# Work of VectorE moved within a layer: bonus factors, low halves, value LoRA shift, mod sums and the banks of the output projection

## The reference, cut to what matters

```python
for l in range(DEPTH):                                  # DEPTH = 2
    mod = (silu(c) @ w_mod[l] + b_mod[l])               # 6 vectors of 1024
    sh1, sc1, gt1, sh2, sc2, gt2 = split(mod, 6)
    h = rmsnorm(x, norm1_g[l]) * (1 + sc1) + sh1
    z = h @ w_cat                                       # layer 1 has 32 more columns: the value LoRA
    ya = rglru_branch(z[LX], z[LY], ...)                # A: conv, gated linear recurrence
    yb = diff_attention(z[Q], z[K], z[V], ...)          # B: rope, two softmax maps
    yc, v_first = rwkv7_mix(z[RW], ..., zvd=z[VD], ...) # C: below
    merged = (sigmoid(z[0:D]) * (ya @ w_merge_a[l]) + sigmoid(z[D:2*D]) * (yb @ w_merge_b[l])
              + sigmoid(z[2*D:3*D]) * (yc @ w_merge_c[l]))
    x = x + gt1 * (merged @ w_out[l])
    h2 = rmsnorm(x, norm2_g[l]) * (1 + sc2) + sh2
    u = causal_dwconv(h2 @ w_up, conv_w, conv_b)        # width 3, 6144 channels
    x = x + gt2 * ((gelu(u[gate]) * u[val]) @ w_down)
return rmsnorm(x, final_g)

# in rwkv7_mix, layer 1: the value's mix with that of layer 0
v = v + (v_first - v) * sigmoid(v0 + token_shift_mix(zvd, v_mu) @ v2)
out = wkv7_scan(r, decay, k, v, -kk, kk * a)            # the state
out = groupnorm(out) * lnx_g + lnx_b
bonus = sum(r * k * r_k, per head) * v
y = (out + bonus) * g
```

## Time and profile before

| | |
|---|---|
| time, median of 3 executions | 1196.32 us (1192.1 to 1197.6) |
| profiled execution: its own time | 1199.33 us |
| its span in the trace | 1197.5 us |
| TensorE busy | 1151.9 us (96%) |
| VectorE busy | 842.9 us (70%) |
| ScalarE busy | 567.7 us (47%) |
| GpSimd busy | 60.2 us (5%) |
| HBM read | 212.01 MB |
| mean granted TensorE clock | 0.978 |

### The profile page before, as it was taken

How to read it: one execution, slowest core, us unless ns; L and a number is a source line. 1 busy time by engine, 2 the same in 40 slices (tenths; PEclk the granted TensorE clock), 3 DMA queues, 4 the chain that set the end, 5 groups by cost and what they waited for, 6 DMA issues and landing times.

```text
span 1197.5 us, 24198 instructions
## 1 busy us (share of the span) xinstructions
PE 1151.9 (96%) x10160; PEld 1043.8 (87%) x10160; DVE 842.9 (70%) x1246; ACT 567.7 (47%) x867; POOL 60.2 (5%) x104
## 2 busy tenths in 40 slices
PE   6999999999999999999999899999999999999997
PEld 6889888888788999999988698778887889999996
DVE  5468988477475788885535679876765767888763
ACT  2236547622264666652331274575124556666532
POOL 0000010003000000001000000000030000000000
PEclk9799999999999999998999899999999999999999
DMA  9956454234135466667725435441521545445650
GB/s 378 297 204 217 176 177 189 94 142 143 72 141 212 156 242 218 227 226 278 281 85 186 173 142 189 156 183 72 199 86 71 189 190 184 175 178 187 225 184 36
DMA packets 40951, 214.34 MB, mean 179 GB/s; under 512 B 7680, under 2 KB 8064, under 8 KB 21536
## 3 DMA queue, kind: packets, MB, share of 16 engines
q1 hardware_dynamic: 29344, 171.13, 39.0%
q0 software_dynamic: 11520, 41.95, 10.0%
HBM read 212.01 MB, written 1.05 MB: 178 GB/s over the span
## 4 chain that ended last, share of the span: by engine, by line
PE 83%; DVE 11%; issue 3%; DMA 3%; ACT 1%; SPq 0%; DVEq 0%; ACTq 0%
PE ps L1587 13%; PE ps L1589 13%; PE ps L1588 13%; PE ps L1600 8%; PE ps L1762 6%; PE ps L1760 6%; PE ps L1766 6%; PE ps L1864 4%; DVE RLO L1091 2%; DMA mring<-wmod_dram 2%; PE ps L1558 2%; PE ps L1565 2%; DVE macc L987 2%; PE ps L1549 1%; PE ps L2040 1%
## 5 line engine op out<-in xcount | busy, mean ns | idle before, releaser
L845 ACT ACTIVATE WH<-ring 128x1024 fp32r<-128x1024 f32 x144 | 151.6, 1058 | 185.7 <-PE ps L1589 170.0
L1459 DVE TENSOR_TENSOR WLO<-ring,WH 128x1024 fp32r<-128x1024 f32 x144 | 175.1, 1223 | 91.2 <-ACT WH L845 91.2
L1587 PE MATMUL ps<-HH,WH 128*128 128x256 f32 x736 | 208.3, 283 | 0.0
L1588 PE MATMUL ps<-HL,WH 128*128 128x256 f32 x736 | 208.3, 283 | 0.0
L1589 PE MATMUL ps<-HH,WLO 128*128 128x256 f32 x736 | 208.3, 283 | 0.0
L1587 PEld LDWEIGHTS ps<-HH,WH 128*128 128x128 f32 x736 | 141.3, 192 | 0.0
L1588 PEld LDWEIGHTS ps<-HL,WH 128*128 128x128 f32 x736 | 141.3, 192 | 0.0
L1589 PEld LDWEIGHTS ps<-HH,WLO 128*128 128x128 f32 x736 | 141.3, 192 | 0.0
L1587 PE MATMUL ps<-GH,WH 128*128 128x256 f32 x384 | 110.6, 288 | 0.0
L1588 PE MATMUL ps<-GL,WH 128*128 128x256 f32 x384 | 109.4, 285 | 0.0
L1589 PE MATMUL ps<-GH,WLO 128*128 128x256 f32 x384 | 109.4, 285 | 0.0
(11 more groups left out here) (383 smaller groups left out, 2494.5 us busy)
## 6 DMA issues: line engine op xcount, KB each, us to landing
ring<-wmain_dram SPq DMA_DIRECT2D x150, 1024.0 KB, 4.8
mring<-wmod_dram POOLq DMA_DIRECT2D x80, 512.0 KB, 5.0
G<-wmod_dram SPq DMA_DIRECT2D x3, 1024.0 KB, 7.8
R<-wmod_dram SPq DMA_DIRECT2D x3, 1024.0 KB, 15.6
TK<-wmod_dram SPq DMA_DIRECT2D x2, 1024.0 KB, 20.7
X<-x_t_dram SPq DMA_DIRECT2D x1, 1024.0 KB, 9.8
SW<-small_dram SPq DMA_DIRECT2D x2, 512.0 KB, 12.6
y_dram<-H SPq DMA_DIRECT2D x4, 256.0 KB, 2.2
```

Source lines behind the costliest of these rows:

```text
L845: A(WH[:, n % 2, part], ring[:, b, part], ACT.Copy).then_inc(hi_ready, 1)
L1459: V.tensor_tensor(WLO[:, n % 2, part], ring[:, b, part], WH[:, n % 2, part].bitcast(F32), ALU.subtract).then_inc(lo_ready, 1)
L1587: MM(out, w_high[:, at], high, start=start, stop=False, skip_group_check=True)
L1588: MM(out, w_high[:, at], low, start=False, stop=False, skip_group_check=True)
```

## The change

- In the preamble VectorE takes block 15 itself (`DIRECT` loses it), reads sum 0 before block 14 instead of after 15, and reads sum 1 ahead of the sixth column of H instead of the fourth. The matmuls that nobody reads are five ahead of `mod_sum(0)` and five ahead of `mod_sum(1)` (they were 2, 2 and 3 in three places).
- The shift of the value LoRA in layer 1 moves ahead of the shift of V.
- The factors of the bonus and of the norm leave the attention part and come in the state chain, behind the chunk of step c = 0 and of step c = 1. The low halves of pairs 16 to 19 each move one rotation forward, the two mod blocks too, and two of them move behind the first four chunks.
- `FILL_READ` is 12.
- The output pairs take banks 0 to 3 in the order of their number.
- In the down stage of layer 0 the sums 5, 6 and 7 come behind other pairs (2, 4 and 9 instead of 0, 3 and 10), and one mod block moves.

```diff
+    if OU <= k < UP:
+        return [k - OU]
     return [g % 4]
...
-FILL_TURN, FILL_READ, FILL_CHAIN, FILL_OUT, FILL_NORM = 8, 8, 4, 6, 8
+FILL_TURN, FILL_READ, FILL_CHAIN, FILL_OUT, FILL_NORM = 8, 12, 4, 6, 8
...
-DIRECT = (3, 7, 11, 15)
+DIRECT = (3, 7, 11)
 UP_BLOCKS = [0] * 4 + [1, 0] * 10
-DN_BLOCKS = [[2, 2, 2, 2, 1, 1, 1, 1, 1, 1, 0, 0], [1, 1, 1, 1, 1, 1, 1, 1, 0, 0, 0, 0]]
-DN_SUMS = [{0: 5, 3: 6, 10: 7}, {8: 11}]
+DN_BLOCKS = [[2, 2, 2, 2, 2, 1, 1, 1, 1, 0, 0, 0], [1, 1, 1, 1, 1, 1, 1, 1, 0, 0, 0, 0]]
+DN_SUMS = [{2: 5, 4: 6, 9: 7}, {8: 11}]
...
             for n in range(FIRST):
+                if n == FIRST - 2:
+                    mod_vector(0)
                 if n not in DIRECT:
                     mod_block(n)
-            mod_vector(0)
...
-                    if (n, m) == (0, 4):
+                    if (n, m) == (0, 6):
                         mod_vector(1)
...
                 half_pairs_low(2, 4)
+                if l:
+                    dve.wait_ge(zv_up, 2)
+                    zv = RT[0:32, :]
+                    V.tensor_tensor(YB[0:32, 2, 1:S], zv[:, 0:S - 1], zv[:, 1:S], ALU.subtract).then_inc(step, tick(n_step))
+                    V.tensor_scalar(YB[0:32, 2, 0:1], zv[:, 0:1], -1.0, None, ALU.mult).then_inc(step, tick(n_step))
+                    after()
+                    V.scalar_tensor_tensor(YB[0:32, 2, :], YB[0:32, 2, :], PR[0:32, l, COL["vmu"]:COL["vmu"] + 1], zv,
+                                           ALU.mult, ALU.add).then_inc(zv_ready, 1)
...
                 mod_vector(6 * l + 2)
                 if l:
-                    dve.wait_ge(zv_up, 2)
-                    zv, zd = RT[0:32, :], Acol
-                    V.tensor_tensor(YB[0:32, 2, 1:S], zv[:, 0:S - 1], zv[:, 1:S], ALU.subtract).then_inc(step, tick(n_step))
-                    V.tensor_scalar(YB[0:32, 2, 0:1], zv[:, 0:1], -1.0, None, ALU.mult).then_inc(step, tick(n_step))
-                    after()
-                    V.scalar_tensor_tensor(YB[0:32, 2, :], YB[0:32, 2, :], PR[0:32, l, COL["vmu"]:COL["vmu"] + 1], zv,
-                                           ALU.mult, ALU.add).then_inc(zv_ready, 1)
...
-                    if b == 0:
-                        dve.wait_ge(lora_act, 10 * (l + 1))
-                        dve.wait_ge(bon_ready, 2 * (l + 1))
-                        for j in range(4):
-                            V.scalar_tensor_tensor(BON[:, j, :], BON[:, j, :], col(l, "lnb", j), GG[:, j, :], ALU.add, ALU.mult).then_inc(gg_ready, 1)
-                        dve.wait_ge(gg_ready, 8 * l + 4)
-                        for j in range(4):
-                            V.tensor_scalar(GG[:, j, :], GG[:, j, :], col(l, "lng", j), None, ALU.mult).then_inc(gg_ready, 1)
+                    if b < 2:
+                        half_pairs_low(16 + 2 * b, 18 + 2 * b)
                     if 0 < b < 3:
-                        half_pairs_low(14 + 2 * b, 16 + 2 * b)
-                    if b:
                         mod_beside(2)
...
                 dve_chunks(0, 4)
+                mod_beside(2)
                 read_scores(0)
...
                         dve_chunks(26 + c, 27 + c)
+                    if c == 0:
+                        dve.wait_ge(lora_act, 10 * (l + 1))
+                        dve.wait_ge(bon_ready, 2 * (l + 1))
+                        for j in range(4):
+                            V.scalar_tensor_tensor(BON[:, j, :], BON[:, j, :], col(l, "lnb", j), GG[:, j, :], ALU.add, ALU.mult).then_inc(gg_ready, 1)
+                    if c == 1:
+                        dve.wait_ge(gg_ready, 8 * l + 4)
+                        for j in range(4):
+                            V.tensor_scalar(GG[:, j, :], GG[:, j, :], col(l, "lng", j), None, ALU.mult).then_inc(gg_ready, 1)
...
-                    keep_clock(2, 5, X[:, 0, :])
+                    keep_clock(5, 5, X[:, 0, :])
                     mod_sum(0)
-                    keep_clock(2, 5, X[:, 0, :])
                     mod_direct(11)
-                    keep_clock(3, 5, X[:, 0, :])
-                    mod_direct(15)
+                    keep_clock(5, 5, X[:, 0, :])
                     mod_sum(1)
...
                     if a == 0:
-                        emptied(g, g % 4)
+                        emptied(g, j)
...
                         down(1, q)
+                        if 4 + q in DN_SUMS[l]:
+                            mod_sum(DN_SUMS[l][4 + q])
```

More of the change, by code:

```diff
@@ L359, in residual_ps @@
         def residual_ps(g, j, i):
-            return ps[:, 5, 0:S] if (j, i) == (3, 1) else ps[:, g % 4, i * S:(i + 1) * S]
+            return ps[:, 5, 0:S] if (j, i) == (3, 1) else ps[:, banks_of(g)[0], i * S:(i + 1) * S]
         def duo(b):
@@ L549, in squares @@
                         g = PAIRS * ((n - 1) // 2) + (OU if n % 2 else PAIRS - 4) + m // 2
-                        act.wait_ge(bank_free[g % 4], EMPTIED[g][g % 4] + 1)
+                        at = banks_of(g)[0]
+                        act.wait_ge(bank_free[at], EMPTIED[g][at] + 1)
                     A(H[:, m, :], X[:, m, :], ACT.Square).then_inc(x_sq, 1)
@@ L1448, in residual @@
                         V.scalar_tensor_tensor(X[:, m, :], residual_ps(g, j, i), scale[:, m:m + 1], X[:, m, :],
-                                               ALU.mult, ALU.add).then_inc((x_tile, bank_free[g % 4])[i], 1)
+                                               ALU.mult, ALU.add).then_inc((x_tile, bank_free[banks_of(g)[0]])[i], 1)
                 g0 = PAIRS * l + UP
```

## The result

| | before | changed |
|---|---|---|
| median | 1196.96 us (1192.1 to 1201.09, 4 executions) | 1216.41 us (1211.54 to 1218.47, 4 executions) |
| ratio | | 1.0158, 95% interval 1.0108 to 1.0209 |
| profiled execution, own time / span | 1199.33 / 1197.5 us | 1217.9 / 1216.1 us |
| mean granted TensorE clock | 0.978 | 0.962 |
| TensorE busy | 1151.9 us | 1169.6 us |

The forecast was 1183.3 us; the kernel became 19 us slower. Of the cases written down it is rival 4: the state chain dropped to the half clock, and stayed there nearly to its end. The rival had been given 0.05.

A forecast was written before the change was run, and what follows sets the result against it. TensorE was taken as the bound (83% of the chain of waits); gains and losses 4.5 + 7.0 - 7.0 + 0 + 0.3 + 8.2 = 13.0 us less, from a median of 1196.32 to 1183.3 us, range 1175 to 1192.

The forecast's parts named there:

- rival 4: State chain, once dropped, stays at 1.2 GHz until the norm; 20 us added to the forecast, 1203 us; chance 0.05.
- State chain: FILL_READ 12 makes TensorE wait 1.9 and 1.8 us for chunks' low halves: 3.5 us a layer, 7.0 us lost.
- rival 3: Each of the four new state chain waits drops the clock for about 6.7 us, half chain: 1190 us; chance 0.12.
- Value LoRA: Layer 1, shift moved ahead: TensorE's wait only changes its name, to the read of a sum; 0 us.
- Down stage: Layer 0, sums 6 and 7 behind other pairs: no late-block wait and less half clock; 8.2 us gained.
- Attention part: Both layers: TensorE's waits for low halves go, until VectorE is late next; 2.8 and 4.2, 7.0 us gained.
- together I put 3.2 us there in place of the 2.42: Attention part: VectorE's waits for DMA and ScalarE after the move, 3.2 us against 2.42 us before.
- Preamble: VectorE adds block 15, so the first product starts at 33.1 with the clock full; 4.5 us gained.
- rival 1: The preamble keeps the half clock, gaining 0.8 us at best there: 1187 us; chance 0.28.
- Banks: Output pairs: out(0) starts earlier, then VectorE is late for out(1); 0.3 us gained in layer 0, none in layer 1.
- The chain's small waits left the clock full: State chain: the argument written against rival 4, whose chance was 0.05.

The follow-up runs named there:

- after_early: The changed kernel, FILL_READ still 12, with the low halves of chunks 26 to 29 made one step of the chain earlier: 1183.60 us, ratio 0.9922.
- before_value: The kernel before with only the value LoRA's shift ahead of the V shift and the read of mod sum 8 right behind it: 1188.36 us, ratio 0.9956.
- before_bonus: The kernel before with only the eight bonus and norm factor instructions moved from the first rotation to the state chain: 1185.49 us, ratio 0.9954.
- before_banks: The kernel before with only the output pairs in banks 0 to 3 in order, and their readers: 1191.43 us, ratio 0.9978.
- before_read12: The kernel before with FILL_READ 12 instead of 8 alone: 1213.84 us, ratio 1.0156.
- before_attention: The kernel before with the whole attention edit: bonus instructions in the state chain, low halves of pairs 16 to 19 and mod blocks moved: 1190.35 us, ratio 0.9984.
- before_preamble: The kernel before with only the preamble's edit: 1192.50 us, ratio 1.0013.
- after_read10: The changed kernel with FILL_READ 10 instead of 12: 1193.12 us, ratio 0.9994.

## Why the prediction was wrong, step by step

- **State chain: 7.0 us of loss forecast, 27 to 32 measured; this is the step that failed.** The waits themselves were read rightly: 1.9 and 1.8 us forecast, 1.91 and 1.71 measured, in both layers. The term "7.0 us lost" priced these waits alone and put the clock behind them at nothing. The reason given was that the clock had stayed full at the waits in layer 0's attention part. That reading is right but left out layer 1 of the same trace, where the wait of 2.03 us at the first gate chunk was followed by 3.4 us at half clock:

```profile
757.83 0.47 PE L1760 MATMUL ps<-WC,HG 128*128 128x512 f32 x1 [2.03 <-DVE RLO L1205]
```
```profile
758.80:762.10 3.30, 3.30 (x12) 2.37 (x12) 2.18 (x2) 0.00 (x0) 0.00 (x0) 0.50 0.34 128
```

And the price was taken from places with wide matmuls behind the wait. Behind this one come the state's small matmuls, eight at a time, with four wide ones between. The runs show the price by itself. By the ratios `FILL_READ` 12 costs 18.6 us in the kernel before (1.0156) and 27 us in the changed one (1.0158 against 0.9930); by the medians it is 1213.8 - 1192.9 = 21 us and 1216.4 - 1183.9 = 32 us. Without the wait (after_early) no loss is to be seen. The Trainium skill, "TensorE: Matmul & The Clock Gate", section "HAM oscillation — how this bites in real kernels", says that a wait for DMA can bring the array back to its cold clock. I weighed it for 6.7 us at each place (rival 3), and for longer in rival 4; the traces show such a fall behind a wait for VectorE, at 303.6 and 897.9 us, and stretches of 23.9 and 30.7 us behind it.
- **Value LoRA: 0 forecast, 0 measured.** Right, with its reason: the wait is 4.61 us and names line 996. Both conditions together gave 5.3 us in before_value (0.8 to 9.5).
- **Down stage: 8.2 forecast, 5.4 by itself (6.4 in the two traces).** The mechanism was right: sum 6 has no wait and takes 1.84 us, and the squares' sum 1.89 for 3.59, as the rows below show. A reason for the size is that one execution stood for the kernel: the trace of before had 6.7 us at half clock behind sum 6. Of the six other traces with the old places of the sums, three have 3.4 us there (before_bonus, before_banks, before_read12) and three have none (before_attention, before_preamble, before_value). The 3.4 us at the squares' sum are in all seven.

```profile
565.73 1.84 PE L1564 MATMUL ps<-sm,macc 128*128 128x1 f32 x16
...
603.82 1.89 PE L1571 MATMUL ps<-H,ones 128*128 128x256 f32 x8
```

- **Attention part: 7.0 forecast, about 2 measured by the times (not clear of nothing), 3.4 by the two traces.** The step that failed is "together I put 3.2 us there in place of the 2.42": VectorE waited 0.87 + 0.88 + 4.23 = 6.0 us. That the bonus factors alone would give 5.5 is not in the prediction at all.
- **Preamble: 4.5 forecast, 1.4 by the starts of the first product, and nothing that the two comparisons of times can tell.** Two things failed. One profiled execution stood for the kernel, and it was the latest of ten at this place. And the five wide matmuls were to keep the clock full, but in the changed kernel it fell at 25.6 us, as rival 1 had it:

```profile
25.60:32.40 6.80, 6.80 (x24) 5.90 (x24) 6.53 (x12) 0.00 (x0) 1.20 (x2) 0.50 1.04 409
```

- **Banks: 0.3 forecast**, and right by the traces: 1.38 us of wait in front of the first output pair against 1.12 in front of the second, for the low half that the prediction named. The times gave 2.6 us with an interval that holds both nothing and 0.3.
- **Sum.** Without the state chain's 7.0 the forecast gain was 20.0 us; the change without `FILL_READ` 12 gained 8.4 by its ratio. So the other terms were too good by about 12 us together, and the one step too low by 27 - 7 = 20. Together that is the 32 us between the forecast gain of 13 and the measured loss of 19.
- **The chances.** The case that came had 0.05. Each sign for it was in the text: the chain's matmuls are narrow, they wait for VectorE, and 12.7 us in the preamble had stayed at half clock over such work. "The chain's small waits left the clock full" was counted against it, although the chain's own waits on VectorE, by the same view of the kernel before, are a fifth of the new one's 1.9 us:

```profile
PE ps L1952 <- DVE TK L1385: 0.7, 2, 0.4
```

What stays open: why the stretch ends when it does (13.6 to 30.7 us behind the same wait); whether the bonus instructions, harmless by themselves, make it longer once it is there (27 us against 18.6 by ratios whose intervals overlap); whether the clock falls in only some executions of after_read10. And it was not tested what makes this place so much dearer than others, the small matmuls behind the wait or those ahead of it. The clock fell behind the wait in all six cases ahead of the state chain (after, before_read12 and after_read10, two layers each), for 10.2 us or more. At the waits of 1.7 to 2.4 us in the attention part it fell in some cases and not in others (not behind the 1.89 us of the changed kernel in layer 1 or the 2.41 us of after_early in layer 0; for 3.4 us behind 2.09 us in before_attention, layer 1).

## What to carry to other kernels

Before moving filler work ahead of a dependency chain, look at which of the remaining pieces opens a new input, and have that input made one step earlier: with no wait the same order of matmuls cost nothing that the times show here, and with a wait of 1.9 us it cost 27 to 32 us in two layers. Price a wait by its place, and look at every such wait in the trace, not at one layer's: ahead of a chain of small matmuls it cost several times its own length through the clock (14 to 18 us a layer, of which 4 us are waits). An edit that pulls work of another engine forward pays only if that work's own inputs (here the mod blocks' DMA) are there by then; and a stretch at half clock in one trace is not a property of the kernel until a second trace has it.

## What the runs showed of the hardware that I had not expected

- The granted clock stayed at 0.50 for 23.9, 30.7 (twice) and 13.6 us while TensorE was recorded busy in all of that time (after and before_read12). Being busy by the record did not bring it back at once.
- Ahead of the state chain the stretch was shorter behind the shorter idle: 1.26 us of idle, 10.2 us at half clock; 1.91 us of idle, 13.6 to 30.7 us. Elsewhere the idle did not tell it: the 4.5 us at the value LoRA had 10.2 us (in the trace of before), and 1.25 us at 292.2 us, ahead of 64 matmuls of 64x64, had none.
- With one and the same preamble the first product started anywhere from 32.0 to 37.6 us, by where in it the clock fell: at 24.7 to 25.6 us in the four traces that started at 37.2 to 37.6, and at 29.4 to 31.0 in the six that started at 32.0 to 35.2.
